# One line of TensorE's program: the seven double steps of an RWKV-7 stage, written out or run as a hardware loop

## The reference

```
def step(S, inp):
    r_t, d_t, k_t, v_t, kk_t, b_t = inp
    sa = jnp.einsum('bhvk,bhk->bhv', S, kk_t)
    S = S * d_t[:, :, None, :] - sa[..., None] * b_t[:, :, None, :] + v_t[..., None] * k_t[:, :, None, :]
    return S, jnp.einsum('bhvk,bhk->bhv', S, r_t)
s_fin, y = lax.scan(step, s0.astype(jnp.float32), xs)
...
out = ((yn + bonus.reshape(B, T, D)).astype(h.dtype) * g) @ p['wo']
```

## Time and profile before

| | us |
|---|---|
| median of 3 runs | 3621.87 |
| lowest and highest run | 3621.57, 3625.8 |
| the profiled execution, its own time | 3621.87 |
| its span in the trace | 3620.3 |
| lane stage, about | 545 to 975 of the span |

### The profile page before, as it was taken

One profiled execution on the slowest core, in us unless ns is written; L12 is line 12 of the kernel. 1 busy time (PEld: TensorE's weight loads), 2 busy tenths in 40 slices (PEclk: granted clock), 3 DMA queues, 4 the chain that ended last, 5 costly groups with the idle time before them and its releaser, 6 DMA issues.

```text
span 3620.3 us, 82690 instructions
## 1 busy us (share of the span) xinstructions
PE 3420.9 (94%) x32728; PEld 3132.6 (87%) x32728; DVE 1735.6 (48%) x2885; ACT 1425.8 (39%) x2287; POOL 42.2 (1%) x81
## 2 busy tenths in 40 slices
PE   6799988988799999999999979999998999999997
PEld 2598877877698999999999968899898999999997
DVE  1634436666545444444444455644645444545453
ACT  1333325555425323323333365433435434333342
POOL 0000000000000000000000000000000000000000
PEclk8899999999999999999999989999999999999999
DMA  9576750000375777777777722233243444445452
GB/s 356 203 282 261 276 190 16 17 17 15 118 272 218 280 279 282 282 281 281 280 281 281 280 100 96 100 134 117 100 134 119 166 168 157 168 157 169 156 174 79
DMA packets 181321, 664.45 MB, mean 184 GB/s; under 512 B 21190, under 2 KB 21360, under 8 KB 180496
## 3 DMA queue, kind: packets, MB, share of 16 engines
q1 hardware_dynamic: 177840, 652.27, 49.6%
q0 software_dynamic: 3296, 9.48, 0.8%
HBM read 657.58 MB, written 4.09 MB: 183 GB/s over the span
## 4 chain that ended last, share of the span: by engine, by line
PE 90%; DMA 3%; DVE 3%; issue 2%; ACT 1%; SPq 0%; DVEq 0%; POOL 0%; ACTq 0%; POOLq 0%
PE ps L1580 23%; PE ps L1582 22%; PE ps L1581 22%; PE ps L1673 6%; PE ps L1564 5%; DMA sb_raw<-stream 2%; PE ps L1680 2%; PE ps L1627 2%; PE ps L1965 1%; PE ps L1963 1%; PE ps L1964 1%; PE ps L1654 1%; PE ps L1996 1%; PE ps L1995 1%; PE ps L1574 0%
## 5 line engine op out<-in xcount | busy, mean ns | idle before, releaser
L973 DVE TENSOR_TENSOR sb_wlo<-sb_raw,sb_whi 128x1024 fp32r<-128x1024 f32 x778 | 940.9, 1223 | 1124.8 <-ACT sb_whi L566 1108.3
L566 ACT ACTIVATE sb_whi<-sb_raw 128x1024 fp32r<-128x1024 f32 x778 | 814.2, 1058 | 1430.8 <-DMA sb_raw<-stream 828.3
L1580 PE MATMUL ps<-sb_ah,sb_whi 128*128 128x288 f32 x3728 | 1119.4, 300 | 41.8 <-DVE sb_al L1052 19.0
L1581 PE MATMUL ps<-sb_ah,sb_wlo 128*128 128x288 f32 x3728 | 1106.7, 297 | 0.0
L1582 PE MATMUL ps<-sb_al,sb_whi 128*128 128x288 f32 x3728 | 1102.5, 296 | 0.0
L1580 PEld LDWEIGHTS ps<-sb_ah,sb_whi 128*128 128x128 f32 x3728 | 705.3, 189 | 76.4 <-issue 64.4
L1582 PEld LDWEIGHTS ps<-sb_al,sb_whi 128*128 128x128 f32 x3728 | 708.7, 190 | 0.0
L1581 PEld LDWEIGHTS ps<-sb_ah,sb_wlo 128*128 128x128 f32 x3728 | 706.7, 190 | 0.0
L1580 PE MATMUL ps<-sb_bh,sb_whi 128*128 128x288 f32 x2048 | 609.3, 298 | 0.0
L1581 PE MATMUL ps<-sb_bh,sb_wlo 128*128 128x288 f32 x2048 | 604.1, 295 | 0.0
L1582 PE MATMUL ps<-sb_bl,sb_whi 128*128 128x288 f32 x2048 | 602.1, 294 | 0.0
(11 more groups left out here) (257 smaller groups left out, 3269.1 us busy)
## 6 DMA issues: line engine op xcount, KB each, us to landing
sb_raw<-stream SPq DMA_DIRECT2D x1226, 512.0 KB, 5.8
sb_x<-xT SPq DMA_DIRECT2D x1, 2304.0 KB, 15.8
sb_x<-xT POOLq DMA_DIRECT2D x1, 2304.0 KB, 9.7
yT<-sb_x SPq DMA_DIRECT2D x1, 2304.0 KB, 6.9
sb_lwa<-lw POOLq DMA_DIRECT2D x16, 130.0 KB, 2.9
sb_lwg<-lw POOLq DMA_DIRECT2D x16, 130.0 KB, 2.4
sb_l1g<-l1g SPq DMA_DIRECT2D x2, 1024.0 KB, 15.0
wkvT<-sb_st POOLq DMA_DIRECT2D x16, 64.0 KB, 2.3
```

Of the source, the lines that this page charges most:

```text
L566: nc.scalar.activation(whi[:, q % SPL, :], raw[:, n % RAW, :], ACT.Copy).then_inc(hi_ready, 1)
L973: nc.vector.tensor_tensor(wlo[:, q % SPL, :], raw[:, n % RAW, :], whi[:, q % SPL, :], ALU.subtract).then_inc(lo_ready, 1)
L1580: mm(out, wh, xh, start=start, stop=False)
L1581: mm(out, wl, xh, start=False, stop=False)
```

## The change

In TensorE's program the Python loop over the turns becomes a call of `rounds`, so the body is in the program once and is run seven times with a register `it` that goes from 0 to 6. Wait targets that depend on the turn are now computed from the register.

```diff
             beside(0, 0, None, 0)
-            for it in range(NITER - 1):
-                turn(it)
+            rounds(pe, 0, NITER - 1, turn)
             beside(1, NITER - 1, 0, NITER - 1)
             beside(None, 0, 1, NITER - 1)
```

## The result

| us | before | after |
|---|---|---|
| median, 5 runs each | 3625.8 (3621.57 to 3627.33) | 3644.23 (3641.65 to 3647.8) |
| ratio | | 1.0055, 95% interval 1.0041 to 1.007 |
| profiled execution, span | 3621.87, 3620.3 | 3649.86, 3648.3 |
| from the second to the sixteenth chain row of L1680 x40 | 374.16 | 397.76 |

The kernel became slower by 18.4 us. Between the profiled executions it is 28.0 us. 4.4 of them lie ahead of the first chain row (545.91 and 550.28 us), where the change does nothing. 0.8 lie between the first and the second (573.61 and 578.77 us), where the loop's first turn begins. 23.6 lie in the fourteen periods behind that, -1.7 from there to the output product (980.30 - 947.77 = 32.5 us before, 1007.34 - 976.53 = 30.8 after), and 1.0 after it. The medians are the better measure of the whole, the fourteen periods of what the loop did.

A forecast was written before the change was run, and what follows sets the result against it. It took the lane stage's PE, DVE and ACT cycle plus late instruction blocks as the bound; +12.0 + 15.0 + 1.4 - 9.1 - 1.5 = +17.8 us on 3621.87 gave 3640 us, own range 3633 to 3648, 8 in 10 3616 to 3656.

The forecast's parts named there:

- (a): At the branch back, before level 5: the loop's first block is gone and refetched, 2.0 us exposed, six times, +12.0 us.
- (b): In the carries behind each branch: the block after the head is asked for late, 2.5 us, six times, +15.0 us.
- (c): On PE's sequencer: 33 more instructions per turn, mostly hidden, 0.2 us per turn, +1.4 us.
- (d): Block boundaries stop moving, so irregular stalls go: -9.1 us in the loop; positions shift behind it, -1.5 us.
- the 7 us of the earlier trace: Near 596.05 us: the next instruction packet started 7 us after PE passed a boundary; taken as support for (b).
- only the head is late: Rival, chance 0.27: behind a branch the next block's fetch follows at once, (b) is nothing; +2.8, 3624.7 us.
- 5.7 us argument: Between level 5 and the carries there are 5.7 us for the next block's packet; counted against (b).
- The sign that the prediction gave for (b): If the period holding the branch is longer by 2 and not by 4.5 us, (b) falls.
- Held: Rival, chance 0.10: all the loop body's blocks stay, no packets after the first turn, faster at 3610.7 us.
- More than one late block or register waits: Rival, chance 0.18: a fixed boundary stalls each turn about 1 us, or registers cost 1 us per turn; 3655 us.

The follow-up runs named there:

- e9: The changed kernel's loop with its head at a block's start and two of five chunks of each level's matmuls left out: 3624.02 us, single run.
- e12: e9 with the branch back announced at the top of each round: 3592.46 us, single run.
- e4: The changed kernel's loop with its branch back moved to just before the carries, nothing announced: 3650.22 us against 3624.82 before.
- e3: The changed kernel's loop with one more instruction at the top of each round that announces the branch back: 3632.83 us against 3624.82 before.
- e6: The changed kernel's loop, unannounced, its head at place 226 of a block, so the first boundary comes after 30 instructions: 3672.91 us against 3627.48 before.
- e2: The kernel before, seven turns written out, with the turn number in a register and waits against computed values, no branch: 3626.87 us against 3624.82.
- e5: The changed kernel's loop with the branch announced and the head at place 194 of a block, the branch late in its block: 3629.30 us against 3627.48 before.
- e7: The changed kernel's loop, unannounced, head at place 7 of a block, putting boundaries where the kernel before had stalled: 3646.27 us against 3627.48 before.
- e8: The changed kernel's loop with its head at a block's start and four of five chunks of each level's matmuls left out: 3581.81 us, single run.
- e1: The changed kernel's loop as three rounds of two turns, the seventh written out, two branches back instead of six: 3632.24 us against 3624.82 before.

## Why the prediction was right

The forecast was 3640 us and the measurement 3644.23. The kernel is slower, as forecast, by 0.41 to 0.70%, which is beyond the 0.2% that the prediction took as what can be told. That the number is so near is luck: a forecast term of 15 us was not there, and one of about 14 us that was not foreseen stood in its place. By its terms, in the profiled executions:

| term | forecast | measured |
|---|---|---|
| (a) the branch misses its block | +12.0 | 20.2 - 6 x 0.57 = +16.8 |
| (b) the next block late in the carries | +15.0 | 0 |
| a lower clock behind each branch | not foreseen | about +14 |
| (c) and (d) in the loop | -7.7 | about -7.5 |
| (d) behind the loop | -1.5 | -1.7 |
| sum | +17.8 | +21.9 |

With the 5.2 us ahead of the second chain row and the 1.0 at the end these are the 28.0 us of the profiled executions; the medians differ by 18.4.

**(a) was right in kind and 0.8 us short each time.** 9.2 blocks are not kept, and e9 to e12 show the limit of eight that made it so. The lead of the sequencer was as counted: the branch starts at 675.3, and level 4's last matmul by the same working at 675.22 + 0.57 = 675.8 (the prediction had 666.3 and 666.7). But the head's packet started 0.92 to 1.04 us behind the start of the branch at four of the six, and 1.47 and 1.58 us at the last two, and not 0.45. The one row behind the 0.45 was too little to go by. In e4 it is 0.93 to 1.04 us at all six, with no other instruction fetch under way, so the microsecond is not a wait for the block next in line (whether the half more at the last two is one stays open). Where the announcement has the head asked for at the boundary (e3), the packet no longer waits for the branch. And from packet to PE it was 2.7 to 2.9 us at five branches (676.33 to 679.27 at the second) and 3.4 at the third, not 2.5 to 2.8. The upper bound is mis-added too: 0.3 + 0.45 + 2.8 less 0.57 is 3.0 and not 3.2, and two branches cost 3.05 and 3.12 us.

**(b) failed.** The forecast carried the 7 us of the earlier trace rows over to the block behind the head. After a branch its packet starts 0.3 to 0.8 us behind PE's restart, and in this loop its boundary is 115 instructions and some 7 us away. The rival "only the head is late" had this right. Its own 5.7 us argument was the one to believe. But the step was a matter of distance and not of kind: with the boundary 30 instructions from the head (e6) or some 20 (e4) the second wait is there, 2.0 to 2.4 us in all but one round. The sign that the prediction gave for (b) would have missed this. It said that (b) falls if the period with a branch is longer by 2 us and not by 4.5. That period is longer by 5.3 us, and (b) is nothing all the same: only the missing wait "issue" in the carries tells.

**The clock took (b)'s place in the sum.** I priced a wait as its own length. All six waits (2.99 to 3.69 us) were followed by a lower granted clock: in the 7 or 8 us behind them it is 0.76 to 0.79 at three branches and 0.57 at three. Its price is a remainder: 397.76 less the 16.8 of (a), and less 366.7 for 14 periods without either (8 x 26.13, and 6 x 26.27, which is e3's 26.58 less its 0.31 us of extra idle), is 14.3 us. By branch it goes with how long the clock stayed low: 1.5 and 1.7 us at the two with 3.4 us at the lower level, 2.5 to 3.3 at the four with 6.8. That fits, since a stretch at half the clock can lose at most half of its length, 1.7 and 3.4 us. e3's shorter waits cost 1.4 to 1.7 us by the same working, with 3.4 us each. The fall in the first turn gives the price without any branch: from the first to the second chain row the changed kernel took 28.49 us and e3, with the same matmuls and no fall, 26.92, 1.6 us less.

That the length of the wait goes with the fall at a branch is shown within e3. It is not the whole rule. In e2, in e5 and in the changed kernel's first turn the clock fell behind waits of 0.62 and 1.77 us that stand in every second period, mostly without a fall, and in before it stayed at 1.00 behind the 2.47 us of the earlier trace rows. What decides these is open.

**(c)** is small (e2: +2.1, -0.7 to +5.8, two falls of the clock included). **(d)** is there in size: seven of the eight periods without a branch are 26.08, the last 26.53. Its reason was only half right. Boundaries that stand still do make the periods alike within a turn's place, but e7 shows one that stalled twice and then no more, and e5 and e6 have fixed boundaries with 26.4 and 26.9 us.

**The rivals.** "Held" was the right alternative to weigh, and eight blocks against 9.2 decided it; e8 and e12 show what it looks like. For the full body no run has it, since 311 instructions would have to go. "More than one late block or register waits" has its second late block only in the kernels built for it: e4, near its 3655, and e6, far above.

No version here beats the kernel before: the nearest, e5, ties with it. The written-out turns already fetch each block once and in line, and the loop adds fetches out of line unless its body fits. What it gives in return here, periods that are alike, is worth less (about 7.5 us).

## What to carry to other kernels

Count a loop's body in blocks of 256 instructions before writing it as a loop: here up to seven blocks ran for 0.21 us per branch, eight only with the branch announced, and beyond that each branch cost 3.3 to 4.0 us on the sequencer and 4 to 5 us on the path (e1, and the changed kernel). If the body is too long, announce the branch, let it stand late in its block and keep the first boundary far from the head; this took 18.4 us of loss down to about 2. Price a wait of PE of over 2 us with what the clock does afterwards, not by its length alone: here 1.4 to 3.3 us more.

## What the runs showed of the hardware that I had not expected

- After idle of 2.12 to 3.69 us at a branch TensorE's granted clock fell in each case of after and e3 (0.57 to 0.79 in the stretches read behind them); after 0.88, 1.45 and 1.49 us it did not. But it also fell, for 3.4 us, behind the standing waits of 0.62 and 1.77 us, once in after, twice in e2, once in e5.
- From the start of a taken branch to the packet of its block it is 0.9 to 1.0 us at four of six branches of after and at all six of e4, where no other instruction packet had started for 4.8 us. An announced block's packet started between 1.5 us before the branch and 0.1 us behind its start in e3.
- An announcement nine blocks ahead of its branch is not lost. It redirects the fetch at the last boundary, and its cost is a late block at the loop's exit: 2.1 us (e3), 2.7 (e12), 3.2 (e5).
- A body of 2007 instructions in exactly 8 blocks was fetched again in every round, and with one instruction more, the announcement, never again (e9, e12).
